# Recurrences of a two-block model: value products ahead of the next unit's preparation, sums and decays a level sooner, gated units without own pairs

## The reference, cut to what matters

```python
def hgrn2_chunk_scan(q, k, v, logf, s0):      # block 1, chunks of 64 in the reference
    ...
        cum = jnp.cumsum(gb, axis=2)
        diff = cum[:, :, :, None, :] - cum[:, :, None, :, :]
        decay = jnp.exp(jnp.where(within_scan, diff, -jnp.inf))
        scores = jnp.einsum('bhtsd,bhsd->bhts', qb[:, :, :, None, :] * decay, kb)
        o = scores @ vb + (qb * jnp.exp(cum)) @ s
        last = cum[:, :, -1:, :]
        s_new = jnp.exp(last[:, :, 0, :])[..., None] * s + jnp.einsum('bhsd,bhse->bhde', kb * jnp.exp(last - cum), vb)
    ...
def gla_chunk_scan(q, k, v, log_g, state0, with_output):   # block 2, the same with
    ...                                                    # gate = log_sigmoid(...) / 16
```

## Time and profile before

| | |
|---|---|
| median of 3 runs | 3601.88 us (3598.09 to 3606.87) |
| the profiled execution, its own time | 3593.62 us |
| its span | 3591.7 us, 49289 instructions |
| TensorE matmuls busy | 3326.5 us (93%), mean granted clock 0.968 |
| VectorE busy | 1996.3 us (56%) |
| ScalarE busy | 1133.2 us (32%) |
| chain that ended last, by engine | TensorE 78%, VectorE 12%, ScalarE 5%, issue 3% |

### The profile page before, as it was taken

How to read it: one execution, slowest core, us unless ns; L and a number is a source line. 1 busy time by engine, 2 the same in 40 slices (tenths; PEclk the granted TensorE clock), 3 DMA queues, 4 the chain that set the end, 5 groups by cost and what they waited for, 6 DMA issues and landing times.

```text
span 3591.7 us, 49289 instructions
## 1 busy us (share of the span) xinstructions
PE 3326.5 (93%) x18504; PEld 2893.9 (81%) x18504; DVE 1996.3 (56%) x3103; ACT 1133.2 (32%) x1476; POOL 130.6 (4%) x64
## 2 busy tenths in 40 slices
PE   6899999989989999999888879999999988889998
PEld 3599999978778877888677757999999766568887
DVE  6556342548856658884567574653433467653334
ACT  2221211245541123223433263311212343543223
POOL 3000000000000000000111100000000111100000
PEclk9899999999999999999989899999999988999999
DMA  5234332321122234553120111333322211113322
GB/s 212 98 118 140 117 140 71 123 88 36 36 93 76 76 113 175 192 196 104 61 71 25 36 42 59 106 129 128 129 92 66 79 42 36 48 47 101 98 95 94
DMA packets 101990, 339.97 MB, mean 95 GB/s; under 512 B 10351, under 2 KB 21487, under 8 KB 100432
## 3 DMA queue, kind: packets, MB, share of 16 engines
q1 hardware_dynamic: 82888, 301.91, 24.7%
q10 hardware_dynamic: 18952, 36.01, 2.9%
HBM read 323.73 MB, written 14.16 MB: 94 GB/s over the span
## 4 chain that ended last, share of the span: by engine, by line
PE 78%; DVE 12%; ACT 5%; issue 3%; DMA 2%; ACTq 1%; POOL 0%; DVEq 0%; SPq 0%
PE ps L424 62%; PE ps L466 3%; PE ps L1034 2%; PE ps L450 2%; DVE u_P L1192 1%; ACT pr L2265 1%; DMA hyena_k<-fst 1%; PE ps L1723 1%; PE ps L1010 1%; PE ps L1710 1%; PE ps L1358 1%; DVE u_Z L1176 1%; PE ps L1051 1%; PE ps L2201 1%; ACT pT L2272 1%
## 5 line engine op out<-in xcount | busy, mean ns | idle before, releaser
L517 ACT ACTIVATE wr_hi<-raw 128x1024 fp32r<-128x1024 f32 x388 | 411.7, 1061 | 601.0 <-PE ps L424 548.4
L527 DVE TENSOR_TENSOR wr_lo<-raw,wr_hi 128x1024 fp32r<-128x1024 f32 x348 | 426.1, 1225 | 100.4 <-ACT wr_hi L517 69.1
L424 PE MATMUL ps<-xx_hi,wr_hi 128*128 128x512 f32 x1056 | 418.0, 396 | 0.5 <-ACT ff_gate L842 0.4
L424 PE MATMUL ps<-xx_lo,wr_hi 128*128 128x512 f32 x1056 | 413.5, 392 | 0.0
L424 PE MATMUL ps<-xx_hi,wr_lo 128*128 128x512 f32 x1056 | 413.4, 391 | 0.0
L890 DVE TENSOR_TENSOR ff_raw<-ps,ff_gate 128x768 f32<-128x768 f32 (+1 forms) x88 | 72.6, 825 | 577.5 <-PE ps L424 572.4
L424 PE MATMUL ps<-xa_hi,wr_hi 128*128 128x384 f32 x1344 | 341.1, 334 | 0.0
L424 PE MATMUL ps<-xa_lo,wr_hi 128*128 128x384 f32 x1344 | 340.9, 334 | 0.0
L424 PE MATMUL ps<-xa_hi,wr_lo 128*128 128x384 f32 x1344 | 340.9, 334 | 0.0
L571 DVE CUSTOM_DVE_ANT_0 ps<-raw,cb 128x1024 f32<-128x1024 f32 x240 | 295.3, 1230 | 51.9 <-DMA raw<-in_mod_stream 35.0
L424 PE MATMUL ps<-hid_hi,wr_hi 128*128 128x384 f32 (+1 forms) x1056 | 316.2, 353 | 3.8 <-DVE H L951 2.1
(11 more groups left out here) (396 smaller groups left out, 5234.5 us busy)
## 6 DMA issues: line engine op xcount, KB each, us to landing
raw<-in_stream SPq DMA_DIRECT2D x392, 512.0 KB, 3.6
raw<-in_mod_stream SPq DMA_DIRECT2D x168, 512.0 KB, 4.4
hK<-hyena_k ACTq DMA_DIRECT2D x4, 1152.0 KB, 6.1
h_kept<-H ACTq DMA_DIRECT2D x2, 2048.0 KB, 9.1
hyena_k<-fst ACTq DMA_DIRECT2D x14, 256.0 KB, 8.5
H<-in_h ACTq DMA_DIRECT2D x1, 3072.0 KB, 9.7
h_kept<-H ACTq DMA_DIRECT2D x1, 3072.0 KB, 9.9
H<-h_kept ACTq DMA_DIRECT2D x1, 3072.0 KB, 10.2
```

The source lines that it names most:

```text
L424: last = pe.matmul(gslot(slot)[:, col:col + n], w, rhs[part], start=(bi == 0 and pi == 0), stop=(bi == len(blocks) - 1 and pi == 2))
L517: act.activation(wr_hi[:, s, :], raw[:, s % RAW, :], ACT.Copy).then_inc(tile_hi, 1)
L527: dve.tensor_tensor(wr_lo[:, s, :], raw[:, s % RAW, :], wr_hi[:, s, :], ALU.subtract).then_inc(tile_lo, 1)
```

## The change

What it does:

- On TensorE the value products come straight after level 6 and its fill, before the next unit's transposes. The fill is shared over eight places; the eighth is behind the transposes.
- On VectorE the write of level 6 comes before `head`, and the add to `oacc` behind it. `head` now also makes Z of level 0, and seam 1 stands behind the scaled keys. Z of level 1 and seam 3 come before the state sums.
- The next unit's sums (`dve_cum`) move from `ahead(6)` to `ahead(5)` on VectorE; on ScalarE the decays move out of `act_unit_head` at level 6 to `ahead(5)`, and the log or soft gate moves a level up. Exp 1 moves into `act_unit_head`.
- A seam is one subtraction with one sign for both halves; ScalarE takes the exp in two instructions of half the width, one with the sign turned.
- Gated units form no own pairs. Once per layer, the products q·k are summed over each head by a 0/1 matrix `blkf` on TensorE, spread over the head's rows, and times 2v they start `oacc2`; P is cleared in units 0 and 2. The gate's product moves from level 1 to level 0.

```diff
         def pe_between(pe, tally, kinds, li):
             steps = KC * len(kinds)
-            for step in range(steps * li // len(LEVELS), steps * (li + 1) // len(LEVELS)):
+            shares = len(LEVELS) + 1
+            for step in range(steps * li // shares, steps * (li + 1) // shares):
                 pe_x_step(pe, tally, step % KC, kinds[step // KC])
...
             bw = U["bw"]
             order = chunk_order(bw)
-            items = [(0, j) for j in range(nsub)]
-            for j in range(nsub):
-                r = slice(j * HD, (j + 1) * HD) if nsub == 2 else slice(0, P)
+            if nsub == 1:
                 place = tally.place("misc_done")
                 pe.wait_ge(misc_free[place], tally.free("misc_done"))
                 m = mslot(place)
                 for c in range(nch):
                     cc = slice(c * CH, (c + 1) * CH)
-                    last = pe.matmul(m[:, cc], k[r, cc], q[r, cc], start=True, stop=True)
+                    last = pe.matmul(m[:, cc], k[:, cc], q[:, cc], start=True, stop=True)
                 last.then_inc(misc_done, 1)
                 tally.passed("misc_done")
...
                 tally.passed("misc_done")
                 ahead(li)
             place, pairs_read = tally.place("misc_done", 1), tally.read("misc_done")
-            ktok_next = head()
-
             pe.wait_ge(misc_free[place], pairs_read)
             place = tally.place("misc_done")
             pe.wait_ge(misc_free[place], tally.free("misc_done"))
                                          skip_group_check=True)
             last.then_inc(misc_done, 1)
             tally.passed("misc_done")
+            ktok_next = head()
+            ahead(len(LEVELS))
             return ktok_next
         def act_decays(act, tally, U, scale):
...
             act.wait_ge(decay_ready, tally.next("decay_ready"))
         def act_level(act, tally, U, li, toks, scale):
-            act.wait_ge(ex_in, tally.next("ex_in", 2))
-            x = U["ex"][li % 3][:, 0:toks]
-            act.activation(x, x, ACT.Exp, scale=scale).then_inc(ex_out, 1)
-            act.wait_ge(ex_out, tally.next("ex_out"))
+            act.wait_ge(ex_in, tally.next("ex_in"))
+            x = halves(U["ex"][li % 3][:, 0:toks], LEVELS[li])
+            for h in range(2):
+                sign = 1.0 if h != U["bw"] else -1.0
+                act.activation(x[:, :, h, :], x[:, :, h, :], ACT.Exp, scale=sign * scale).then_inc(ex_out, 1)
+            act.wait_ge(ex_out, tally.next("ex_out", 2))
         def act_unit_head(act, tally, U, toks, scale):
-            act_decays(act, tally, U, scale)
             act_level(act, tally, U, 0, toks, scale)
+            act_level(act, tally, U, 1, toks, scale)
             ms = tally.take("misc_done")
             act.wait_ge(misc_done, tally.now("misc_done"))
             act.activation(U["ktok"][:, :], mslot(ms)[:, 0:NT], ACT.Copy).then_inc(misc_free[ms], 1)
             act.wait_ge(misc_free[ms], tally.read("misc_done"))
         def act_unit(act, tally, U, nsub, toks, scale, ahead):
-            tally.passed("misc_done", nsub + 1)
+            tally.passed("misc_done", 2 if nsub == 1 else 1)
             at_level = []
             for li in range(len(LEVELS)):
-                if li:
+                if li > 1:
                     act_level(act, tally, U, li, toks, scale)
                 at_level.append((tally.take("misc_done"), tally.now("misc_done"), tally.read("misc_done")))
                 if li - 2 in BLOCK_LEVELS:
                     act_put(act, tally, U, li - 2, nsub, toks, *at_level[li - 2])
+                if li == len(LEVELS) - 1:
+                    tally.passed("misc_done")
                 ahead(li)
-            tally.passed("misc_done")
         def act_put(act, tally, U, li, nsub, toks, ms, done, read):
...
             a = cum[:, :, 1, 0:1] if U["bw"] else cum[:, :, 0, b - 1:b]
-            a = a.broadcast_to([P, n, b])
-            first, second = cum[:, :, 0, :], cum[:, :, 1, :]
-            if U["bw"]:
-                upper, lower = (first, a), (a, second)
-            else:
-                upper, lower = (a, first), (second, a)
-            dve.tensor_tensor(x[:, :, 0, :], *upper, ALU.subtract).then_inc(ex_in, 1)
-            dve.tensor_tensor(x[:, :, 1, :], *lower, ALU.subtract).then_inc(ex_in, 1)
-            tally.passed("ex_in", 2)
+            a = a.unsqueeze(2).broadcast_to([P, n, 2, b])
+            dve.tensor_tensor(x, cum, a, ALU.subtract).then_inc(ex_in, 1)
+            tally.passed("ex_in")
+
+        def dve_make_z(dve, tally, U, q, k, li, toks):
+
...
+            qh, kh = halves(q[:, 0:toks], b), halves(k[:, 0:toks], b)
+            left, right = (qh, kh) if U["bw"] else (kh, qh)
+            dve.tensor_tensor(z[:, :, 0, :], x[:, :, 0, :], left[:, :, 0, :], ALU.mult).then_inc(z_ready, 1)
+            dve.wait_ge(ex_out, tally.next("ex_out"))
+            dve.tensor_tensor(z[:, :, 1, :], x[:, :, 1, :], right[:, :, 1, :], ALU.mult).then_inc(z_ready, 1)
+            tally.passed("z_ready", 2)
         def dve_unit_head(dve, tally, U, q, k, toks):
             dve_seam(dve, tally, U, 0, toks)
-            dve_seam(dve, tally, U, 1, toks)
             dve.wait_ge(decay_ready, tally.next("decay_ready"))
             dve.tensor_tensor(U["ek"][:, :], U["ek"][:, :], k[:, :], ALU.mult).then_inc(ke_ready, 1)
             dve.wait_ge(ke_ready, tally.next("ke_ready"))
+            dve_seam(dve, tally, U, 1, toks)
             dve.tensor_tensor(U["eq"][:, 0:toks], U["eq"][:, 0:toks], q[:, 0:toks], ALU.mult).then_inc(dve_step, 1)
             dve.wait_ge(dve_step, tally.next("dve_step"))
-
-        def dve_unit(dve, tally, U, q, k, nsub, toks, oacc, ahead, head):
+            dve_make_z(dve, tally, U, q, k, 0, toks)
+
+        def dve_unit(dve, tally, U, q, k, nsub, toks, oacc, ahead, head, clear=False, after_first=lambda: None):
             bw = U["bw"]
...
                 dve.copy_predicated(dst, mk.broadcast_to([P, nsub, nch, HD // b, b]), src).then_inc(misc_free[ms], 1)
                 dve.wait_ge(misc_free[ms], tally.read("misc_done"))
-            for j in range(nsub):
+            if nsub == 1:
                 ms = tally.take("misc_done")
                 dve.wait_ge(misc_done, tally.now("misc_done"))
-                dve.tensor_tensor(chunks(U["P"][:, j, 0:toks]), chunks(mslot(ms)[:, 0:toks]),
+                dve.tensor_tensor(chunks(U["P"][:, 0, 0:toks]), chunks(mslot(ms)[:, 0:toks]),
                                   ident[:, :].unsqueeze(1).broadcast_to([P, nch, CH]), ALU.mult
                                                 ).then_inc(misc_free[ms], 1)
                 dve.wait_ge(misc_free[ms], tally.read("misc_done"))
-            make_z(0)
+            elif clear:
+                dve.memset(U["P"], 0.0).then_inc(p_clear, 1)
+                dve.wait_ge(p_clear, tally.next("p_clear"))
             dve_seam(dve, tally, U, 2, toks)
+            dve_make_z(dve, tally, U, q, k, 1, toks)
+            dve.wait_ge(z_ready, tally.now("z_ready", -2))
+            dve_seam(dve, tally, U, 3, toks)
             ms = tally.take("misc_done")
             dve.wait_ge(misc_done, tally.now("misc_done"))
...
-                    src = U["Z"][:, 1, c * P:(c + 1) * P]
+                    src = add_rows[:, :]
                     dve.tensor_tensor(halves(src, HD), halves(add[:, c * P:(c + 1) * P], HD),
                                       blk[:, :].unsqueeze(1).unsqueeze(3).broadcast_to([P, 1, 2, HD]), ALU.mult).then_inc(dve_step, 1)
...
                     dve.wait_ge(z_ready, tally.now("z_ready", -2))
                     dve_seam(dve, tally, U, li + 2, toks)
                 ahead(li)
                 put(li - 1)
+            put(nl - 1)
             if head is not None:
                 head()
-            put(nl - 1)
-            if head is not None:
-                tally.take("misc_done")
             ms = tally.take("misc_done")
             dve.wait_ge(misc_done, tally.now("misc_done"))
-            if not bw:
+            if nsub == 1 and not bw:
                 ins = dve.tensor_copy(oacc, mslot(ms)[:, 0:toks])
             else:
                 ins = dve.tensor_tensor(oacc, mslot(ms)[:, 0:toks], oacc, ALU.add)
             ins.then_inc(misc_free[ms], 1)
             dve.wait_ge(misc_free[ms], tally.read("misc_done"))
+            if head is not None:
+                tally.take("misc_done")
...
                 def ahead(li, nxt=u + 1, u=u, hy0=at_hy):
                     if u == 7 and li == 1:
                         hy_tile(hy0 - 1)
+                    if nxt < 8 and li == 4:
+                        act_log_forget(act, tally, nxt)
                     if li == 4:
                         hy_tile(hy0)
                     elif li == 6 and HY_TILES[u] == 3:
                     elif nxt < 8 and li == 3:
                         split_tile(act, tally)
                     elif nxt < 8 and li == 5:
-                        act_log_forget(act, tally, nxt)
```

(49 more changed lines are left out.)

37 lines of the change are left out of this document (19 added, 18 removed).

## The result

The changed kernel takes 3626.2 us (median; 3624.9 to 3629.7), the kernel before, beside it, 3598.2: a ratio of 1.0080, 95% interval 1.0064 to 1.0095, so slower by 28 us. The forecast was 3600 with 3578 to 3618.

A forecast was written before the change was run, and what follows sets the result against it. TensorE was taken as the fullest engine, with VectorE nearly as full in the first recurrence. Terms 33 - 21.5 - 13 = -1.5 us on the profiled execution of 3593.6; with the median 8.3 higher, forecast 3600 us, range 3578 to 3618.

The forecast's parts named there:

- First recurrence: Its 8 units: exponential 6 queued behind decays and sums adds 22 us, slower TensorE clock 11; +33 (22 to 39).
- All of its signs: First recurrence: units 31 to 35 us apart, TensorE waits 4 us or more before level 6, clock 0.5 behind it.
- the loop's sum: First recurrence, one unit's loop between own-pair writes: steps summed to 32.4 us, now 28.85.
- Gated layers: Two gated recurrences: layer 0 gains 21.5 us (-27 to -16), layer 1 gains 13 (-18 to -6).
- own pairs gone, new products: Gated units: small matmuls leave, 10.6 us in layer 0 and 7.0 in layer 1; new products add 3.2 each.
- waits, fill, clock: Gated layers: waits fall 10.5 and 2.9 us, moved fill saves 2.2 each, clock gives back 1.4 and 4.
- Clock and fill: Gated layers: fewer gaps return 1.4 and 4 us of clock; fill moved behind the last value products saves 2.2 each.
- New products: Gated layers, before the first transposes: two products of 768 columns, once per layer, +3.2 us.
- Slow clock covers the path: Rival: clock stays down longer, first recurrence costs 40 us, layer 1 wins only 6; +12.5, 3614 us, chance 0.16.
- Slot waits: Rival, layer 0: waits for the gate's PSUM slot and first key copy cost twice; +7, 3609 us, chance 0.09.
- Clock holds: Rival: gaps before level 6 leave the clock up, first recurrence costs 22; -12.5, 3589 us, chance 0.23.
- the change does what it says: Rival: exponential 6 does not wait for the decays, first recurrence gains 8; -42.5, 3559 us, chance 0.10.

The follow-up runs named there:

- e3: Changed kernel with the next unit's running sums, logarithm and decays back at level 6 in the first recurrence alone: 3593.0 us (0.9986).
- e5: Changed kernel with only ScalarE's decays moved behind level 6's exponential in the first recurrence, sums and logarithm still early: 3612.1 us (1.0041).
- e9: Kernel before without own pairs in the gated units, GpSimd's low parts there cut to 128 of 1024 columns, rest left out: 3567.6 us (0.9917).
- e2: Kernel before with GpSimd's low parts in the gated layers cut to 128 of 1024 columns, rest left out: 3576.6 us (0.9936).
- e1: Changed kernel with GpSimd's low parts in the gated layers cut to 128 of 1024 columns, rest left out: 3591.5 us (0.9977).
- e4: Changed kernel with running sums and decays of the next unit back at level 6 in all three recurrences: 3579.6 us (0.9957).
- e11: Changed kernel with all running sums and decays at level 6 and GpSimd's low parts of 128 of 1024 columns, rest left out: 3543.1 us (0.9842).
- e8: Changed kernel with fill shares 6 to 8 of a first-recurrence unit all behind level 5, sums still early: 3612.1 us (1.0040).
- e7: Kernel before without own pairs in the gated units, their values multiplied once ahead of the units, order otherwise old: 3584.1 us (0.9971).

## Why the prediction was wrong

**First recurrence, forecast +33: right, measured +33.** The path too. TensorE's busy time grew from 215.4 to 226.3 us, 10.9, where 11 were put down to the clock (picked between 0 and 17, so its exactness is in part luck); the other 22 are waits. All of its signs came: units 32.4 to 34.4 us apart for the six units with two fill tiles, waits of 3.9 to 4.9 us before level 6, the exponential at the decays' end, the clock at 0.50 behind it. The chain had two links of about equal weight, VectorE's running sum ahead of Z 6 and ScalarE's decays ahead of exponential 6 (20 us each, e3 and e5), where the loop's sum had 3.8 and 2.6 us a unit. It did not tell apart that the rest of the change gains 6.5 us there (e3): +40 and -6.5 make the +33.5.

**Gated layers, forecast -21.5 and -13: wrong, -6.2 and +7.6 between the marks.** By the experiments:

| term | layer 0: forecast | measured | layer 1: forecast | measured |
|---|---|---|---|---|
| own pairs gone, new products | -7.4 | -9.9 | -3.8 | -10.5 |
| waits, fill, clock | -14.1 | -2.3 | -9.1 | +3.3 |
| holds, more than in the old order | 0 | +6.0 | 0 | +14.8 |
| sum | -21.5 | -6.2 | -12.9 | +7.6 |

(First row e9 - e2; second e1 - e9; third (changed - e1) - (before - e2).)

The same terms over the whole kernel, by the medians, are -9.0, +23.9 and +13.2, together +28.1; the forecast had -11.2, +9.8 (with the first recurrence's +33) and 0. So two steps failed, each by about 13 to 14 us of the medians (24 and 21 between the marks); the own pairs' price was right within the error.

- *Holds, a term put at nothing*: the sentence that VectorE "has less to do than before, and it stands ahead of nothing that TensorE waits for". The durations of VectorE that the prediction shows are of the first recurrence, where GpSimd is still (0.00 in the earlier trace rows). The trace of before had the warning, the 1.22 us above for an instruction of 0.56. In the changed kernel holds of 1.9 and 2.1 us fall on the state sums before the gate's product and on the running sum before the decays. The running sum's place is not what makes them dearer: with the sums late again (e4 against e11) they cost as much. Which part of the new order does it, no run separates.
- *Waits*: the layout let them fall by 10.5 and 2.9 us. Measured with the holds, they went from 27.0 to 25.7 and from 24.3 to 25.3. Without the holds the new order takes 6.0 and 3.2 us from TensorE's idle time (e9 to e1, stage less busy time). The sums a level sooner cost 3.5 and 4.7 us between the marks (e1 - e11), where the forecast called them cheap in layer 0 ("Here decays cost little at level 6").
- *Clock and fill*: half of one loss and 4 us of clock were to come back. Instead TensorE's busy time grew by 3.7 and 6.5 us from e9 to e1, with the same 1308 and 892 instructions in the stage (so the fill's 2.2 us did not leave it either), at a clock of 0.90 and 0.86 instead of 0.92. In the changed kernel it is 0.90 and 0.80; in layer 1, changed against e1, 10.1 of the 19.1 us are busy time (132.4 against 122.4), and so clock. There TensorE waits 3.9 and 4.2 us before level 6, and 16 instructions behind such a wait take 1.97 us, 1.11 elsewhere:

```profile
2989.91 1.97 PE L1036 MATMUL ps<-u_Z 64*128 64x64 f32 x16 [3.94 <-DVE u_Z L1160]
...
3000.20 1.11 PE L1036 MATMUL ps<-u_Z 64*128 64x64 f32 x16
```

  These are single profiles; "Open" says how far their clock can be trusted.
- *New products*: +3.2 us forecast in front of the first transposes. The stretches between the recurrences grew by 0.2 us and shrank by 1.5: nothing of them shows. In layer 1 they were priced too high besides: it has 512 columns, and 3.2 us is the price of 768.
- The sign units "at 37 to 39 us" came for the first only: 39.0, then 42.7 and 44.5 in layer 0. The sign of being wrong, "layer 0 above 178", came in the window of the earlier trace rows: 183 (177.8 between the marks).

**Rivals.** "Slow clock covers the path" ended nearest (3614), but by its smaller part: the first recurrence cost 33, not 40; layer 1, which it let win only 6 us, lost 8. "Slot waits" named the right place and in layer 0 the price: the gate's product waits 8.2 us, twice the layout's 4.0. It had not the cause, and put the whole at +7 instead of +28. "Clock holds" fell (8 instructions take 1.97 us behind every wait of 3.9 to 4.9 us), and so did "the change does what it says" (exponential 6 does wait for the decays). No rival had GpSimd.

**Open.** The gated code of layer 0 is the same in the changed kernel, e3, e5 and e8, and takes 177.8 us in the first and 183.9 to 184.0 in the others; TensorE is busy for 153.4 us of it in the first, at a clock of 0.90, and for 163.1 and 163.3 in e3 and e5, at 0.85 and 0.84. The same wait of 2.75 us stands before the same gate's product in both; in the changed kernel the product then takes 2.14 us (above), in e3 2.92:

```profile
1874.21 2.92 PE L1931 MATMUL ps<-lr,gatew 32*128 32x512 f32 x4 [2.75 <-DVE u_S L1226]
```

The profiled executions of e3, e5 and e8 lay 3.9 to 6.4 us above their medians, that of the changed kernel 0.8, so this may well be scatter between executions. A term of the table that is no larger than these 6 us is not shown by one profile; the two failed steps rest on the medians beside it. What decides which stretches run at the upper level there was not tried.

## What to carry to other kernels

Before an instruction is moved ahead of a level's exponential or product, write down both engines' queues in front of that level: a sum that nobody waited for became a wait twice, once on ScalarE and once on VectorE. Where GpSimd works beside VectorE, price a VectorE instruction that reads SBUF with GpSimd's remaining time on top, and see whether it is on the path. Cut what holds VectorE before judging an order: with four pieces the new order with late sums gained 26 us, the old one 3. And set a stage's difference in one profile beside the medians before building on it: e7's gated layers said that the missing own pairs gave nothing, its median said 13 us.

## What the runs showed of the hardware

- A VectorE instruction that reads only SBUF and starts beside GpSimd's subtraction waits for its end and runs then: 2.10 instead of 0.23, 3.02 instead of 0.96; one that reads PSUM kept its 0.28. A product from PSUM and an SBUF operand is among the latter, and so is a masked write from PSUM (0.72 and 1.02 beside GpSimd). One that already ran when GpSimd's began kept its time (0.96).
- GpSimd pays for being cut: 128x1024 takes 2.4 to 3.1 us, four times 128x256 3.1 to 3.5. 128 columns still took 0.5 to 0.9.
- The same subtraction on VectorE takes 1.22 us.
- The lower clock doubles small level products as a whole: 8 instructions 1.00 to 1.97 us after waits of 3.9 to 4.9 us; with the fill moved into the wait (e8) the stage's clock is 0.99 instead of 0.92.
- Behind a wait of 2.75 us the clock differs between executions: the same product took 2.14 us in one profile and 2.92 in another.
